# Quarters of the output panels between the attention heads of the last two mixers

## The chip, the cores and the metric

One core of one Trainium2 chip runs the whole program. The metric is the device time of one execution, in microseconds (us). TensorE multiplies, VectorE and ScalarE do the work between the products, GpSimd helps, and SyncE's queue brings the weights.

## The reference, cut to what matters

Two blocks, one behind the other, on 256 tokens of 1024 channels. The first has four gated feed-forward layers and two mixers, and is not touched. The second has two mixers (`l` = 0 and 1) of this form:

```python
for l in range(DEPTH):
    h = rms_norm(x, norm_g[l])
    proj = h @ w_in[l]
    q_a, k_a, v_a, q_h, f_h, i_h, q_m, z = jnp.split(proj, split_points, axis=-1)
    ...
    o_a = moba_attention(qa, ka, va).reshape(B, S, G)
    ...
    o_h = rms_norm(o_h, hgrn_o_norm[l]).astype(x.dtype).reshape(B, S, G)

    kv_m = rms_norm(mem, mem_norm_g[l]) @ w_mem_kv[l]
    ...
    o_m = memory_attention(qm, km, vm).reshape(B, S, G)

    y = jnp.concatenate([o_a, o_h, o_m], axis=-1) * jax.nn.silu(z)
    x = x + y @ w_out[l]
```

`o_a` is causal attention with 8 heads of 64 channels (`moba`), `o_h` a gated recurrence with 4 heads of 128 (`hgrn`), `o_m` attention to 256 rows of memory with 4 heads of 128 (`matt`).

## The kernel before

**Panels.** All weights come as 226 panels of 128 x 2048 numbers (1 MB), in the order in which they are used. Three slots hold them. SyncE loads panel n when panel n - 3 has been split. ScalarE rounds a panel into `w_hi` (`split_hi`, line 1345), VectorE takes the rest into `w_lo` (`split_lo`, line 1638), and TensorE does each product three times (`three`, lines 897 to 899): hi by hi, lo by hi, hi by lo. A panel of a projection or of an output is 48 such products of 128 x 256; in the very last output (`down_rows`) it is 24 of 128 x 512. `split_hi` of panel n waits until TensorE has used panel n - 3.

**The order of the work.** `order()` writes one list of steps, (engine, kind, arguments), and each engine runs its own steps in the order of this list; semaphores count finished steps. So a step that stands early in the list and waits holds everything behind it on its engine.

**The last mixers.** The input projection `in2_l` has 20 panels (numbers 170 to 189 and 200 to 219), the output `out2_l` 6 (190 to 195 and 220 to 225). Panels 4 to 19 of the projection are cut into halves and woven between the rounds of the recurrence (`level` products, line 1093), of the column norms (`cn_sum` line 1237, `cn_rstd`, `cn_use` lines 1882 and 1884) and of the rotations (`swap` line 1226, `rope`). `BESIDE_2` says behind which round each half stands, counted from the round in which the norms begin. The heads run as a pipeline of rounds, 12 heads, `moba` 0 to 7 and then `matt` 0 to 3. In round r, with the step's lag in brackets:

```python
ATTEND = [("pe", "turn_p", 2), ("pe", "scores", 0), ("pe", "attend", 3), ("act", "p_cols", 2), ("dve", "divide", 1),
          ("dve", "mask_max", 0), ("act", "exp", 0)]
```

`scores` (lines 1250, 1252) goes to a PSUM bank, `mask_max` (VectorE, line 1918 or 1916) scales, masks and finds the maximum, `exp` (ScalarE, line 1545), `divide` (VectorE, lines 1931, 1935), `turn_p` transposes (lines 1262 to 1268), `p_cols` (ScalarE, line 1556) copies back, `attend` (lines 1208, 1209) multiplies by the values. When all heads are done, `gate_out` multiplies by the gate, `y_hi` and `y_lo` split the result, and the six output panels follow as whole panels. Beside the heads of mixer 0 the memory rows of mixer 1 are normed (`sumsq`, `row_rstd`, `scale`); beside those of mixer 1 the residual x is turned into rows (`turn_back` line 1065, `rows_back`).

## Time and profile before

| | |
|---|---|
| median of three runs | 1662.78 us (1659.75 to 1663.9) |
| profiled execution, its own time | 1663.09 us |
| its span, first to last instruction | 1660.7 us |
| TensorE busy | 1574.2 us, 95% of the span, 12086 products |
| TensorE loading weights | 1498.2 us, 90% |
| VectorE busy | 1033.9 us, 62% |
| ScalarE busy | 749.7 us, 45% |
| GpSimd busy | 93.5 us, 6% |
| granted clock, mean over the span | 0.971 |
| chain that ended last | TensorE 80%, VectorE 12%, ScalarE 4% |

Busy times are sums over the execution; the engines work beside each other. A busy TensorE need not be a fast one, so the granted clock of each stretch is read beside it.

### The profile page before, as it was taken

The page shows a single profiled execution, that of the slowest core. Times are in us where ns is not written, and L with a number is a line of the kernel's source. Part 1 is how long each engine was busy: PE and PEld are TensorE (multiplying, and loading weights), DVE is VectorE, ACT ScalarE, POOL GpSimd, SP SyncE. Part 2 cuts the span into 40 slices and gives each one's busy share as a digit, 9 for nine tenths or more (in the row PEclk, how much of TensorE's full clock was granted, in tenths as well). Part 3 has the DMA queues.
Part 4 walks back from the last instruction along what each step waited for, and adds up shares of the span by engine and source line. Part 5 has one row for each costly group of instructions (what it writes and reads, how often), then busy time and mean ns, then how long its engine had stood idle before and what let it go on. Part 6 is the DMA issues. An engine that isn't in the chain of part 4 may idle for free.

```text
span 1660.7 us, 28994 instructions
## 1 busy us (share of the span) xinstructions
PE 1574.2 (95%) x12086; PEld 1498.2 (90%) x12086; DVE 1033.9 (62%) x1234; ACT 749.7 (45%) x890; POOL 93.5 (6%) x66
## 2 busy tenths in 40 slices
PE   6999998998999999999997999999999899899988
PEld 6999998887999999999886899999999679799856
DVE  5555577736755575556576755556686655578644
ACT  4333356325433353333446433335645564554653
POOL 1000000010000000000000100002022001013000
PEclk9999999999999999999999999999999889999979
DMA  6554534204554544555331455544444214424201
GB/s 251 191 185 177 179 126 153 87 17 157 201 179 177 180 173 180 183 188 184 137 143 52 167 195 189 182 177 153 152 159 147 76 52 178 177 102 153 102 1 76
DMA packets 34064, 246.53 MB, mean 148 GB/s; under 512 B 3835, under 2 KB 3963, under 8 KB 4406
## 3 DMA queue, kind: packets, MB, share of 16 engines
q1 hardware_dynamic: 32854, 238.28, 39.8%
q0 software_dynamic: 1120, 6.96, 1.1%
q8 instruction: 68, 1.11, 0.3%
q14 instruction: 22, 0.18, 0.0%
HBM read 244.18 MB, written 1.05 MB: 148 GB/s over the span
## 4 chain that ended last, share of the span: by engine, by line
PE 80%; DVE 12%; ACT 4%; issue 2%; DMA 1%; POOL 0%; DVEq 0%; SPq 0%; ACTq 0%; POOLq 0%
PE ps L897 23%; PE ps L899 23%; PE ps L898 23%; PE ps L1093 4%; DVE w_lo L1638 2%; DVE act_lo L1737 2%; ACT act_hi L1414 1%; DVE x L1696 1%; ACT w_hi L1345 1%; PE ps L1237 1%; PE ps L1208 1%; ACT work L1545 1%; PE ps L1252 1%; PE ps L1226 1%; DVE work L1757 1%
## 5 line engine op out<-in xcount | busy, mean ns | idle before, releaser
L897 PE MATMUL ps<-act_hi,w_hi 128*128 128x256 f32 x2528 | 733.5, 290 | 27.6 <-DVE act_lo L1737 9.0
L898 PE MATMUL ps<-act_lo,w_hi 128*128 128x256 f32 x2528 | 722.0, 286 | 0.0
L899 PE MATMUL ps<-act_hi,w_lo 128*128 128x256 f32 x2528 | 721.7, 285 | 0.0
L1638 DVE TENSOR_TENSOR w_lo<-raw,w_hi 128x2048 fp32r<-128x2048 f32 x225 | 526.1, 2342 | 288.0 <-ACT w_hi L1345 285.5
L1345 ACT ACTIVATE w_hi<-raw 128x2048 fp32r<-128x2048 f32 x225 | 429.2, 1910 | 490.9 <-PE ps L899 484.7
L897 PEld LDWEIGHTS ps<-act_hi,w_hi 128*128 128x128 f32 x2528 | 491.9, 195 | 38.0 <-DVE act_lo L1737 11.0
L898 PEld LDWEIGHTS ps<-act_lo,w_hi 128*128 128x128 f32 x2528 | 492.4, 195 | 3.2 <-issue 3.1
L899 PEld LDWEIGHTS ps<-act_hi,w_lo 128*128 128x128 f32 x2528 | 491.8, 195 | 0.0
L897 PE MATMUL ps<-g_hi,w_hi 128*128 128x256 f32 x704 | 199.4, 283 | 0.0
L899 PE MATMUL ps<-g_hi,w_lo 128*128 128x256 f32 x704 | 199.3, 283 | 0.0
L898 PE MATMUL ps<-g_lo,w_hi 128*128 128x256 f32 x704 | 199.3, 283 | 0.0
L897 PEld LDWEIGHTS ps<-g_hi,w_hi 128*128 128x128 f32 x704 | 135.2, 192 | 0.0
L899 PEld LDWEIGHTS ps<-g_hi,w_lo 128*128 128x128 f32 x704 | 135.2, 192 | 0.0
L898 PEld LDWEIGHTS ps<-g_lo,w_hi 128*128 128x128 f32 x704 | 135.2, 192 | 0.0
L897 PE MATMUL ps<-w_hi,act_hi 128*128 128x256 f32 (+1 forms) x336 | 107.3, 319 | 0.0
L898 PE MATMUL ps<-w_lo,act_hi 128*128 128x256 f32 (+1 forms) x336 | 101.2, 301 | 0.0
L899 PE MATMUL ps<-w_hi,act_lo 128*128 128x256 f32 (+1 forms) x336 | 101.0, 301 | 0.0
L881 POOL TENSOR_TENSOR pair<-pair 128x512 f32<-128x512 f32 x27 | 40.7, 1506 | 905.5 <-ACT pair L1392 904.8
L897 PEld LDWEIGHTS ps<-w_hi,act_hi 128*128 128x128 f32 x336 | 65.3, 194 | 5.8 <-issue 3.6
L898 PEld LDWEIGHTS ps<-w_lo,act_hi 128*128 128x128 f32 x336 | 65.3, 194 | 4.8 <-issue 2.9
L1648 DVE TENSOR_TENSOR pair<-ps,r_b 128x512 f32<-128x512 f32 x44 | 30.4, 690 | 60.4 <-PE ps L899 60.4
L899 PEld LDWEIGHTS ps<-w_hi,act_lo 128*128 128x128 f32 x336 | 65.2, 194 | 1.9
(262 smaller groups left out, 1418.9 us busy)
## 6 DMA issues: line engine op xcount, KB each, us to landing
raw<-panels SPq DMA_DIRECT2D x226, 1024.0 KB, 4.8
table<-tab POOLq DMA_DIRECT2D x1, 1472.0 KB, 11.3
table<-tab POOLq DMA_DIRECT2D x1, 1216.0 KB, 5.8
xn<-x_in SPq DMA_DIRECT2D x1, 1024.0 KB, 5.1
work<-mem_in POOLq DMA_DIRECT2D x1, 1024.0 KB, 10.1
xn<-mem_in POOLq DMA_DIRECT2D x1, 1024.0 KB, 5.4
out<-work POOLq DMA_DIRECT2D x4, 256.0 KB, 2.3
table<-tab POOLq DMA_DIRECT2D x1, 832.5 KB, 6.1
```

The costliest lines, as they stand in the source:

```text
L881: nc.gpsimd.tensor_tensor(pair[:, 0:512], pair[:, 0:512], pair[:, 512 * b:512 * b + 512], ALU.add).then_inc(pool_done, 1)
L897: pe.matmul(o, l[0], r[0], start=start, stop=False, skip_group_check=shared)
L898: pe.matmul(o, l[0], r[1], start=False, stop=False, skip_group_check=shared)
L899: return pe.matmul(o, l[1], r[0], start=False, stop=stop, skip_group_check=shared)
L1093: ins = pe.transpose(oh, lhs(h), ident) if turn else pe.matmul(oh, lhs(h), rhs(h), start=True, stop=True)
L1208: pe.matmul(o, v0, first, start=True, stop=False, skip_group_check=True)
L1226: pe.matmul(ps[:, bank], matrix, values, start=True, stop=True).then_inc(pe_done, 1)
L1237: pe.matmul(ps[:, bank], ones, sq[norm_index[unit] % 2], start=True, stop=True).then_inc(pe_done, 1)
L1345: nc.scalar.activation(w_hi[:, s], raw[:, s], ACT.Copy).then_inc(panel_hi, 1)
L1638: tt(w_lo[:, s], raw[:, s], w_hi[:, s].bitcast(F32), ALU.subtract).then_inc(panel_lo, 1)
L1648: tt(grid(gate_x, 2), grid(ps[:, 4], 2), rb(2), ALU.mult).then_inc(gate_scaled, 1)
L1737: finish(stt(act_lo[:, s], src, gain_col(tag, c), act_hi[:, s].bitcast(F32), ALU.mult, ALU.subtract))
```

## The change

- The first four output panels are cut into quarters (`quarter`: the 12 products, or 6 wide ones, that write one of four banks) and one quarter stands behind the `attend` of each round, from round 3 on in mixer 0 and from round 5 on in mixer 1. The quarters that the rounds have no place for follow behind the last head, then panels 4 and 5 whole.
- The last eight halves of the projection (panels 16 to 19) stand two rounds later, so the last three of them are among the first heads. The splits of the panels that follow them go with them.
- The gates and splits of the output rows (`gate_out`, `y_hi`, `y_lo`) stand as single steps between the heads.
- The norm of the memory rows stands as single steps in several rounds instead of in one.
- To leave banks 0 to 3 for the output, scores of all heads from the fourth on go to bank 4 and their turned probabilities to bank 5, one bank each instead of two.
- x is turned into rows in rounds 3 to 6, in banks 0 to 3.

```diff
-def halves(panels):
...
+def halves(panels, bare=2):
...
     out = []
-    panels = panels[:-2] + [p[:2] for p in panels[-2:]]
+    panels = panels[:len(panels) - bare] + [p[:2] for p in panels[len(panels) - bare:]]
     for (_, _, args), *rest in panels:
         out += [[("pe", "half", (*args, 0))], [("pe", "half", (*args, 1)), *rest]]
     return out
...
 BESIDE_2 = [-13, -13, -12, -12, -11, -11, -10, -10, -9, -9, -8, -8, -7, -7, -6, -6, -5, -5, -4, -4, -3, -3, -2, -2,
-            -1, 0, 1, 2, 3, 4, 5, 6]
+            1, 2, 3, 4, 5, 6, 7, 8]
...
     chains = [rounds(NORM_COLS, [(f"sk{l}", 0), (f"sk{l}", 1)]), hgrn,
               [[]] * n + rounds(NORM_COLS, qk + [(f"ho{l}", 0), (f"ho{l}", 1), (f"sq{l}", 0), (f"sq{l}", 1)]),
               [[]] * (n + 2) + rounds(ROPE, qk),
-              [[]] * (h + 11) + [[("dve", "gate_out", ((f"moba{l}", g),)) for g in (0, 1)]],
               [[]] * h + rounds(ATTEND, [(f"moba{l}", i) for i in range(8)] + [(f"matt{l}", i) for i in range(4)]),
-              [[]] * (h + 13) + [y_splits(l, 0), y_splits(l, 2)]]
+              [[]] * (h + 7) + [[("dve", "gate_out", ((f"moba{l}", 0),))], y_splits(l, 0), [], [],
+                                [("dve", "gate_out", ((f"moba{l}", 1),))], y_splits(l, 2),
+                                [("dve", "gate_out", ((f"matt{l}", 0),))], y_splits(l, 8)],
+              [[]] * (h + 3 + 2 * l) + out_pieces(f"out2_{l}", 0, 4)]
     if l == 0:
         load, *stats = mem_norm(1)
-        chains += [[[]] * (h + 1) + [[load]] + [[]] * 3 + [[s for s in stats if s[0] == "act"]] +
-                   [[s for s in stats if s[1] == "scale"]]]
+        chains += [[[]] * (h + 1) + [[load]] + [[]] * 2 + [stats[0:1], stats[1:3], stats[3:4], stats[4:6], [], stats[6:7], stats[7:8]]]
     if l:
-        chains += [[[]] * (h + 2) + sum(([[("pe", "turn_back", (b,)), ("act", "rows_back", (b,))], []] for b in range(PAIRS)), [])]
+        chains += [[[]] * (h + 3) + [[("pe", "turn_back", (b,)), ("act", "rows_back", (b,))] for b in range(PAIRS)]]
     places = [n + r for r in BESIDE_2]
-    out = weave(merge(*chains), halves(panel_list(f"in2_{l}", None, 4)), places)
-    return (out + late_splits(f"in2_{l}") + [("dve", "gate_out", ((f"matt{l}", g),)) for g in (0, 1)]
-            + y_splits(l, 8) + y_splits(l, 10))
+    out = weave(merge(*chains), halves(panel_list(f"in2_{l}", None, 4), 0), places)
+    return out + [("dve", "gate_out", ((f"matt{l}", 1),))] + y_splits(l, 10)
+
+
+def out_pieces(name, start, stop):
+
+    out = []
+    for (_, _, args), *rest in panel_list(name, None, start, stop):
+        pieces = [[("pe", "quarter", (*args, b))] for b in range(PAIRS)]
+        pieces[-1] += rest
+        out += pieces
+    return out
...
-            out += panel_steps("out2_0", None, 0, 4) + turns + all_columns("mem1") + panel_steps("out2_0", None, 4)
+            out += panel_steps("out2_0", None, 4, 5) + turns + all_columns("mem1") + panel_steps("out2_0", None, 5)
...
         else:
-            out += panel_steps("out2_1")
+            out += panel_steps("out2_1", None, 4)
...
+        def first_three(unit):
+
+            return unit[0].startswith("moba") and unit[1] < 3
+
         def score_bank(unit, m, back=False):
 
 
             i = att_index[unit]
             two = lambda u_: len(atts[u_][0]) == 2
+            if unit[0][0] == "m" and not first_three(unit):
+                return 1 if back else 4
             if back:
                 return 1 if two(unit) or (i and two(att_list[i - 1])) else 2
             return m if two(unit) else i % 2
+
+        def turn_bank(unit):
+
+            return 5 if unit[0][0] == "m" and not first_three(unit) else 2 + att_index[unit] % 2
 
         def spans(full):
...
         def back_bank(b):
-            return bank_of("in2_1", b)
+            return b
...
-            def down(slot, parts, first, last, n, j=None, step=0):
+            def down(slot, parts, first, last, n, j=None, step=0, pairs=range(PAIRS)):
 
                 pe.wait_ge(panel_lo, of(j, n + 1, step))
-                for d in range(DC):
+                for d in range(2 * pairs[0], 2 * pairs[-1] + 2):
                     for c in range(2):
                         o = ps[:, d // 2, SEQ * (d % 2):SEQ * (d % 2) + SEQ]
                         ins = three(o, weight(slot, c, P * d, P, D), [a[:, c, :] for a in parts],
                                     first and c == 0 and d % 2 == 0, last and c == 1, True)
                     if last and d % 2 and d < DC - 1:
                         ins.then_inc(bank_ready, 1)
-                ins.then_inc(panel_used, 1)
-
-            def down_rows(slot, parts, first, last, n):
+                if pairs[-1] == PAIRS - 1:
+                    ins.then_inc(panel_used, 1)
+
...
-            def panel(name, k, parts=(0, 1)):
+            def panel(name, k, parts=(0, 1), pairs=range(PAIRS)):
                 n = BASE[name] + k
                 if name.startswith("out"):
 
+                    if (name, k) == ("out2_0", 0):
+                        b = pairs[-1]
+                        e, kind = ("dve", "mask_max") if b < 2 else ("act", "p_cols")
+                        pe.wait_ge(done[e], at(e, kind, ("moba0", 2 - b % 2)))
+                    if (name, k) == ("out2_1", 0):
+                        pe.wait_ge(act_done, at("act", "rows_back", pairs[-1]))
                     last = {("out0", 0): ("cn_use", ("do", 1)), ("out0", 2): ("cn_use", ("ro", 1)), ("out1", 0): ("cn_use", ("fo", 1)), ("out1", 2): ("gate_out", ("dil", 1))}
                     for l in range(2):
-                        last.update({(f"out2_{l}", 0): ("cn_use", (f"ho{l}", 1)), (f"out2_{l}", 2): ("y_lo", l, 2),
-                                     (f"out2_{l}", 4): ("y_lo", l, 10)})
+                        last.update({(f"out2_{l}", 0): ("cn_use", (f"ho{l}", 1)), (f"out2_{l}", 2): ("y_lo", l, 0), (f"out2_{l}", 3): ("y_lo", l, 2),
+                                     (f"out2_{l}", 4): ("y_lo", l, 8), (f"out2_{l}", 5): ("y_lo", l, 10)})
...
-                    (down_rows if name == "out2_1" else down)(n % SLOTS, parts, k == 0, k == N_OF[name] - 1, n)
+                    (down_rows if name == "out2_1" else down)(n % SLOTS, parts, k == 0, k == N_OF[name] - 1, n, pairs=pairs)
...
+            def quarter_panel(name, k, b):
+                panel(name, k, pairs=(b,))
...
                 if b < 2:
-                    pe.wait_ge(act_done, at("act", "evacuate", "in2_1", 18 + b))
+                    pe.wait_ge(dve_done, at("dve", "mask_max", ("moba1", 2 - b)))
                 else:
-                    pe.wait_ge(act_done, at("act", "rows_back", b - 2))
+                    pe.wait_ge(act_done, at("act", "p_cols", ("moba1", 4 - b)))
...
+                if unit[0].startswith("moba") and unit[1] == 3:
+                    pe.wait_ge(act_done, at("act", "evacuate", "in2_" + unit[0][4], 19))
...
+                back = 1 if turn_bank(unit) == 5 else 2
+                if i >= back:
+                    pe.wait_ge(act_done, at("act", "p_cols", att_list[i - back]))
+                p, bank = probs[:, i % 2, 0], ps[:, turn_bank(unit)]
...
-                if unit[0].startswith("matt") and unit[1] == 0:
-                    pe.wait_ge(dve_done, at("dve", "gate_out", ("moba" + unit[0][4:], 1)))
+                if unit[0].startswith("matt") and unit[1] % 2 == 0:
+                    pe.wait_ge(dve_done, at("dve", "gate_out", ("moba" + unit[0][4:], unit[1] // 2)))
```

What this does to VectorE's order at the head of the heads in mixer 0. In the rows, line 1884 (after: 1917) and the three behind it are the norm of the last pair of the recurrence's heads with its split, 1882 (1915) the norm of a memory query, 1918 (1951) mask_max, 1931 and 1935 (1964, 1968) divide, 1638 (1671) split_lo. Before:

```order
L1884 SCALAR_TENSOR_TENSOR xn<-ps,small,pair 128x512
L1886 TENSOR_TENSOR xn<-xn,work 128x512
L1874 CAST act_hi<-xn 128x512
L1875 TENSOR_TENSOR act_lo<-xn,act_hi 128x512
L1882 SCALAR_TENSOR_TENSOR work<-work,small,pair 128x512
L1918 ISA work,stat<-ps,table 128x128
L1918 ISA stat 128x1
L1918 ISA work,stat<-ps,table 128x256
L1918 ISA stat 128x1
L1882 SCALAR_TENSOR_TENSOR work<-work,small,pair 128x512
L1931 RECIPROCAL stat<-stat 128x2
```

and with the change:

```order
L1671 TENSOR_TENSOR w_lo<-raw,w_hi 128x2048
L1917 SCALAR_TENSOR_TENSOR xn<-ps,small,pair 128x512
L1919 TENSOR_TENSOR xn<-xn,work 128x512
L1907 CAST act_hi<-xn 128x512
L1908 TENSOR_TENSOR act_lo<-xn,act_hi 128x512
L1915 SCALAR_TENSOR_TENSOR work<-work,small,pair 128x512
L1951 ISA work,stat<-ps,table 128x128
L1951 ISA stat 128x1
L1951 ISA work,stat<-ps,table 128x256
L1951 ISA stat 128x1
L1671 TENSOR_TENSOR w_lo<-raw,w_hi 128x2048
L1915 SCALAR_TENSOR_TENSOR work<-work,small,pair 128x512
```

The split_lo of panel 190 now stands ahead of that norm, and the one of panel 191 between the first mask_max and the norm that the first divide stands behind.

VectorE again, two rounds on, the mask of head 2 and the divide of head 2. Before:

```order
L1918 ISA work,stat<-ps,table 128x128
L1918 ISA stat 128x1
L1918 ISA work,stat<-ps,table 128x256
L1918 ISA stat 128x1
L1931 RECIPROCAL stat<-stat 128x2
L1935 TENSOR_SCALAR work<-work,stat 128x128
```

and with the change:

```order
L1951 ISA work,stat<-ps,table 128x128
L1951 ISA stat 128x1
L1951 ISA work,stat<-ps,table 128x256
L1951 ISA stat 128x1
L1671 TENSOR_TENSOR w_lo<-raw,w_hi 128x2048
L1964 RECIPROCAL stat<-stat 128x2
```

The split_lo of panel 192 has come between them.

TensorE in round 5 of mixer 1, from the scores to the step behind attend. Line 1250 and 1252 (after: 1282, 1284) are scores, 1208 and 1209 (1238, 1239) attend, 1065 (1095) a transpose of x, 1262 (1295) the next turn. Before:

```order
L1250 MATMUL ps<-work 128x128
L1252 MATMUL ps<-work 128x256
L1208 MATMUL ps<-work 64x256
L1209 MATMUL ps<-work 64x128
L1262 MATMUL ps<-const,work 128x128
```

and with the change:

```order
L1282 MATMUL ps<-work 128x128
L1284 MATMUL ps<-work 128x256
L1238 MATMUL ps<-work 64x256
L1239 MATMUL ps<-work 64x128
L917 MATMUL ps<-w_hi,act_hi 128x512
L918 MATMUL ps<-w_lo,act_hi 128x512
L919 MATMUL ps<-w_hi,act_lo 128x512
L917 MATMUL ps<-w_hi,act_hi 128x512
L918 MATMUL ps<-w_lo,act_hi 128x512
L919 MATMUL ps<-w_hi,act_lo 128x512
L1095 MATMUL ps<-const,x 128x128 x4
```

Six products of an output panel have come behind attend, and behind them the transposes of x.

## Rows read from the trace of the kernel before

**Rows 1.** Windows: stretch, its length, busy time of each engine, PEclk, DMA share, GB/s

```profile
1312.00:1357.00 45.00, 37.27 (x135) 22.84 (x134) 21.99 (x91) 25.57 (x81) 0.33 (x1) 0.70 0.07 24
1357.00:1393.00 36.00, 36.00 (x304) 36.00 (x303) 23.08 (x23) 18.68 (x20) 0.96 (x1) 1.00 0.48 176
...
1623.00:1656.00 33.00, 32.92 (x146) 26.89 (x144) 17.18 (x14) 10.61 (x8) 1.49 (x3) 1.00 0.20 79
```

**Rows 2.** Timeline of TensorE, mixer 0: start, us, instruction, [idle before, releaser]

```profile
1318.38 0.47 PE L1262 MATMUL ps<-const,work 128*128 128x128 f32 x1 [4.83 <-DVE work L1935]
...
1320.98 0.47 PE L1262 MATMUL ps<-const,work 128*128 128x128 f32 x1
...
1328.74 0.48 PE L1262 MATMUL ps<-const,work 128*128 128x128 f32 x1
...
1356.72 0.47 PE L897 MATMUL ps<-act_hi,w_hi 128*128 128x256 f32 x1
```

**Rows 3.** Windows at low clock, and one with half panels between heads

```profile
881.35:884.76 3.41, 3.41 (x15) 2.58 (x15) 1.00 (x1) 2.69 (x4) 0.00 (x0) 0.50 0.26 103
...
1314.84:1342.14 27.30, 23.64 (x68) 13.88 (x69) 11.97 (x54) 15.81 (x52) 0.00 (x0) 0.50 0.06 23
...
883.00:898.00 15.00, 13.51 (x97) 12.93 (x98) 9.46 (x36) 6.69 (x22) 0.00 (x0) 0.94 0.19 70
```

**Rows 4.** Timeline of TensorE, mixer 1, a round at full clock

```profile
1605.28 0.48 PE L1250 MATMUL ps<-work 64*128 64x128 f32 x2
...
1606.13 0.65 PE L1208 MATMUL ps<-work 128*64 128x256 f32 x2
...
1606.92 0.33 PE L1262 MATMUL ps<-const,work 128*128 128x128 f32 x1
...
1607.31 0.60 PE L1250 MATMUL ps<-work 128*128 128x256 f32 x2
```

**Rows 5.** Timeline of TensorE, mixer 0, first product of the recurrence's output

```profile
1281.22 0.38 PE L1310 MATMUL ps<-work 128*128 128x128 f32 x2
```

**Rows 6.** Timeline of VectorE, mixer 0, end of the levels

```profile
1274.84 1.36 DVE L2044 COPY_PREDICATED work<-table,ps 128x512 f32<-128x512 uint32 x2 [1.80 <-PE ps L1093]
1276.24 2.29 DVE L1638 TENSOR_TENSOR w_lo<-raw,w_hi 128x2048 fp32r<-128x2048 f32 x1
1278.55 0.69 DVE L2046 COPY work<-ps 128x512 f32<-128x512 f32 x1
```

**Rows 7.** Timeline of TensorE, the heads of the first block's second mixer

```profile
880.85 0.33 PE L1262 MATMUL ps<-const,work 128*128 128x128 f32 x1 [3.75 <-DVE work L1939]
```

**Rows 8.** Timeline of VectorE, mixer 0, the first heads

```profile
1312.23 0.75 DVE L1882 SCALAR_TENSOR_TENSOR work<-work,small,pair 128x512 f32<-128x512 f32 x1 [0.77 <-ACT pair L1535]
...
1313.24 0.42 DVE L1918 CUSTOM_DVE_ANT_0 work<-ps,table 128x256 f32<-128x256 f32 x1
...
1317.78 0.55 DVE L1935 TENSOR_SCALAR work<-work,stat 128x128 f32<-128x128 f32 x2
```

**Rows 9.** Timeline of ScalarE, mixer 0, exp of head 0 and the evacuate behind it

```profile
1313.70 0.40 ACT L1545 ACTIVATE work<-work,stat 128x128 f32<-128x128 f32 x1 [1.57 <-DVE stat L1918]
...
1314.86 0.60 ACT L1436 ACTIVATE work<-ps 128x512 f32<-128x512 f32 x1 [0.17 <-ACT work L1545]
```

**Rows 10.** The page, costliest groups: the two splits

```profile
L1638 DVE TENSOR_TENSOR w_lo<-raw,w_hi 128x2048 fp32r<-128x2048 f32 x225 | 526.1, 2342 | 288.0 <-ACT w_hi L1345 285.5
L1345 ACT ACTIVATE w_hi<-raw 128x2048 fp32r<-128x2048 f32 x225 | 429.2, 1910 | 490.9 <-PE ps L899 484.7
```

**Rows 11.** Timeline of TensorE, mixer 1: turn of head 0, first output panel

```profile
1584.19 0.48 PE L1262 MATMUL ps<-const,work 128*128 128x128 f32 x1 [4.83 <-DVE work L1935]
...
1622.88 0.59 PE L897 MATMUL ps<-w_hi,act_hi 128*128 128x512 f32 x1
```

**Rows 12.** Timeline of TensorE, two turns with half a panel between (first block)

```profile
893.64 0.27 PE L1262 MATMUL ps<-const,work 128*128 128x128 f32 x1
...
898.15 0.27 PE L1262 MATMUL ps<-const,work 128*128 128x128 f32 x1
```

28 lines of the change are left out of this document (13 added, 15 removed).

## The prediction

> **What bounds the kernel now.** The page says that TensorE is busy nearly all of the time, so I looked for where it is not, or where busy does not mean fast. The table of stretches shows that at once [rows 1]. While the heads of each of the two last mixers run (1312 to 1357 and, in the same form, 1578 to 1623) the granted clock is only 0.70 and TensorE is idle for 7.7 of 45 us, and the DMA engines move almost nothing (0.07). The stretches behind them, the output panels, are dense: 304 panel products in 36.00 us, so 0.118 us each, and 146 wide ones in 32.92 us, 0.225 us each. So the place to win something is inside the heads' stage, and a panel put there costs TensorE 48 x 0.118 = 5.7 us at full clock.
>
> Then the timeline of TensorE there [rows 2]. It waits 4.83 us for VectorE before the turn of head 0 at 1318.38; the turn of head 1 follows at 1320.98, that of head 3 at 1328.74, and the first output panel starts at 1356.72. The row of the clock [rows 3] gives 27.30 us at 0.50, that is 1.2 GHz, with TensorE busy for 23.64 of them. At full clock, 2.4 GHz, a round's products start 0.39 (turn), 0.85 (scores) and 0.79 us (attend) apart, 2.03 us in all [rows 4]: the lost clock costs some 12 us in each mixer, the idle time some 7 us. What limits a round where TensorE doesn't is the loop mask_max, exp, divide: 1320.98 - 1318.38 = 2.6 us [rows 2], of which mask_max is 0.65 (its second part is the row 1313.24, over at 1313.66), divide 0.75 (its last 0.55 in the row at 1317.78) [rows 8], exp 1.0 (from 1313.70, up to the evacuate at 1314.86 less a hop of 0.17) [rows 9].
>
> **The change, part by part, for the first of the two mixers.** Round r is the one with the scores of head r.
>
> *The projection's last halves two rounds later.* Two halves stood before and behind the last level product. Now nothing stands there, and the state product (row 1281.22 [rows 5]) waits only for VectorE: level_in 6 from 1274.84, a split_lo of 2.29, and the copy of level 7, over at 1279.24 [rows 6]. That is 2.0 us earlier, and TensorE idles in front of it, where it was busy: the last level's products can be over 1 us after level 6 is handed on at 1274.84, so some 3.5 us. After the nearest such gap, 3.75 us [rows 7], the clock was 0.50 for 3.41 us [rows 3]. The same here costs 1.7 us. Together -0.3 us. Bounds: -2.0 if the clock holds, +1.4 if it is low twice as long. The rounds behind it keep their shape (half, column sum, swap), one panel later.
>
> *The split of panel 190 and 191 in VectorE's and ScalarE's order.* The order shows a w_lo ahead of the norm of the last HGRN pair and another behind the first mask_max. The first pushes mask_max by 2.29 less the 0.77 us for which VectorE was idle ahead of row 1312.23 [rows 8]: +1.5. The second sits in the chain to the first turn. Before: mask_max ends at 1313.66, the turn starts at 1318.38, 4.7 us. After: exp 1.0, evacuate 0.6 [rows 9], split_hi 1.9, split_lo 2.3 (means of 1.910 and 2.342 us [rows 10]), the norm use 0.75 (as at 1312.23), divide 0.75 [rows 8], hops 0.3: 7.6 us, +2.9. Sum +4.4 us. Cover gone: before, these two splits lay under panel products on TensorE; queued behind the w_lo are divide of head 0 and all masks after it, and TensorE waits for those. The moved half 19 fills 2.9 us of the wait, and this is no gain, as it was taken from the gap of the step before.
>
> *Rounds 2 to 5.* Before: 1318.38 to 1328.74, 10.4 us. After, from the turn of head 0: mask, exp, divide, mask, exp (3.5 us with hops), evacuate 0.6 and split_hi 1.9, split_lo 2.3, divide 0.75 and hops: the turn of head 2 comes at +10.1, mask_max at +10.75; then scores 0.85, attend 0.8, a quarter of 12 x 0.118 = 1.4 with 0.25 for getting into it: round 5 starts at +14.1. So +3.7 us, with two quarters done. The 0.25 is chosen between nothing and the 0.47 us of the first product of row 1356.72 [rows 2].
>
> *Rounds 5 to the end of the heads.* Before: 1328.74 to 1356.72, 28.0 us. After, if the clock is full: a round of 2.03 + 1.65 = 3.7 us; seven of them with 0.3 for the wider products of the memory heads, 26.3; three without scores, 3.1 + 3.1 + 2.4 = 8.6; and stalls. Each w_lo among the heads (193, 194) is asked for when its slot comes free, at the end of a quarter, and then 1.9 + 2.3 + 0.75 us pass to the next divide. A round hides all but some 1.4 to 1.9 us of it; with a short third wait 3.6 us. Sum 38.5: +10.5 us, with ten quarters done.
>
> *The output panels behind.* Twelve quarters are gone: -12 x 1.42 = -17.0 us.
>
> The first mixer: -0.3 + 4.4 + 3.7 + 10.5 - 17.0 = **+1.3 us**.
>
> The second mixer is the same up to its turn of head 0 (-0.3 + 4.4). From there to the first panel it was 1622.88 - 1584.19 = 38.7 us [rows 11]. Now: 13.2 to round 5 (no quarter yet, two transposes of x of 0.5); two rounds with both, 8.3; one of 3.65; four of 3.75 with the wider heads, 15.1; a stall at split 223, 1.8; 5.9 and 0.9 at the end: 48.9, +10.2 us. Nine quarters of 6 x 0.225 = 1.35 are gone: -12.2. Sum **+2.1 us**.
>
> *At nothing.* The memory norm in single pieces is 4.9 us of ScalarE in four parts, at most 1.3 in a round; p_cols and exp take 1.5 of the 3.7, so the round hides it, and if not, it is 1 us per part. The panel loads start earlier with the splits, on SP's queue alone and while the engines carry 0.07 [rows 1]. The score bank shared by all heads from the fourth on makes scores wait for the mask before it; that mask ends some 2 us before TensorE is back from its quarter. The first quarters' waits (mask_max, p_cols or the copied rows) are on steps a round old. Behind a waiting quarter stands the next turn, and for that ScalarE's p_cols waits.
>
> In sum +3.4 us on the profiled execution's 1663.1: 1666.5. That execution lies 0.3 us over the median of the three runs; I say **1666 us**. The kernel's measurement tells a change of 0.3%, 5 us, from none. The idle time is mostly not removed: the filler hides it, and the splits that feed the filler make it anew in the chain of the heads.
>
> **Rivals.** (1) *The filler comes cheaply.* If the clock holds through the new gap (-1.7 each) and getting into and out of a quarter costs nothing (-0.25 for 21 quarters, -5.2), it is 1658 us. For it speaks a head with half a panel between the dilated heads: 898.15 - 893.64 = 4.51 us [rows 12], of which 24 x 0.118 = 2.83 are the panel, so 1.68 for head and transition, under my 2.28. Against it: those heads use 128-wide operands, these 64-wide ones, and three of my rounds are not TensorE's anyway.
>
> (2) *The clock stays low.* It ends on the slower side. TensorE enters round 2 from a wait of nearly 3 us, as now from one of 4.83. If it stays at 1.2 GHz, each round from the fifth costs 3.7 us more, since both head and quarter double. One such round in each mixer gives 1674 us, three 1689; from half a round in one mixer on, it decides for slower. For it: once low in these stages, it stayed so for 27.3 us with TensorE busy [rows 3]. Against it: no dense panel stood in that stretch, and with half panels between the heads the mean was 0.94 from 883 to 898 [rows 3]. The stalls that I count, four in each mixer, are the other way to it: after each a low stretch of 3.41 us, 1.7 us lost, would be +13.6 us, 1680. The Trainium skill has this as a rule: "TensorE: Matmul & The Clock Gate", section "A second HAM failure mode: psum-queue depth-cycling", says that short idles between groups of products, often enough, make the clock go up and down. By that rule the filler with its stalls would not hold the clock; the trace agrees in part, since the stretch from 883 to 898 had a wait of 1.49 us and lost little.
>
> (3) *ScalarE and VectorE set the rounds.* If every split costs what it does in round 3 (4.2 us instead of some 1.7), three of them add 7 us: 1673. Against it: a round has 1.1 us between 3.7 and 2.6, and turns lag by two rounds. That the quarters end up waiting for their own banks, so that nothing is interleaved, I hold for very unlikely, and count it here.
>
> **Chances.** Forecast as worked out, 0.40, with a range of its own of 1661 to 1671; three quarters of it within 0.3%, the rest slower. Rival 1: 0.25, 0.20 of it faster. Rival 2: 0.25, nearly all slower. Rival 3: 0.10, mostly slower. So faster 0.20, same 0.40, slower 0.40. The range takes in rival 1's figure and one low round per mixer: 1657 to 1678; 0.1 is left below, 0.1 above.
>
> **What will show it.** In the changed profile: a TensorE gap of 3 to 4 us before the state products and 0.50 on the clock behind it; the turn of head 0 some 4 us later against its stage; waits of TensorE for divide of 1.5 to 2.3 us after the w_lo among the heads; rounds of 3.7 us between turns; the last head's attend over near 1374 instead of 1356.7 in the first mixer; the clock of the heads' stage above 0.9. Wrong would be: a clock of 0.5 in filled rounds (then slower), rounds near 3.1 us and no stall at the splits (then faster by several us per mixer), or a longer wait of the quarters than of the turns.

## The result, and the profile after

The changed kernel takes 1674.18 us (median of 4 runs, 1673.17 to 1674.65), the kernel before in the same session 1663.09 us: a ratio of 1.0069, 95% interval 1.0048 to 1.0089. It is 11.1 us slower, by more than the 0.3% that a measurement of this kernel can tell from none. The profiled execution took 1674.13 us with a span of 1672.4, against 1660.7 of before. The forecast was 1666 us, with 0.40 each for no measurable change and for slower: it was 8 us too low, and its range, 1657 to 1678, holds the time.

First the stages that answer to [rows 1] and [rows 3], in the table of stretches of the changed kernel (stretch, its length, busy time of PE, PEld, DVE, ACT, POOL, granted clock, DMA share, GB/s):

```profile
1314.90:1373.90 59.00, 49.11 (x286) 38.87 (x285) 31.69 (x93) 32.83 (x81) 0.00 (x0) 0.88 0.23 87
1373.90:1399.00 25.10, 25.10 (x212) 25.07 (x211) 14.43 (x17) 13.11 (x17) 2.50 (x2) 1.00 0.23 85
1399.00:1407.60 8.60, 4.78 (x23) 4.22 (x23) 7.35 (x3) 3.81 (x5) 5.06 (x2) 0.80 0.65 247
1595.33:1615.81 20.48, 17.25 (x51) 10.38 (x50) 8.36 (x32) 9.90 (x28) 0.00 (x0) 0.50 0.23 88
1646.80:1667.60 20.80, 20.78 (x92) 16.87 (x90) 8.03 (x9) 3.18 (x3) 1.43 (x3) 1.00 0.06 24
```

The stretch of the heads has grown and its clock has risen from 0.70 to 0.88, but TensorE still idles for 9.9 us in it. The third row is new: behind the output panels, where before nothing waited, TensorE is busy for 4.78 of 8.60 us. In the last mixer there is still a stretch of 20.48 us at 0.50.

Next the timeline of TensorE in mixer 0, to be laid beside [rows 2] and [rows 5]: the recurrence's output, then the turns (L1295) of heads 0, 1, 3, 4, 6 and 10 and, between the second and the third of them, the scores (L1282) of head 3.

```profile
1279.71 0.49 PE L1343 MATMUL ps<-work 128*128 128x128 f32 x2 [3.53 <-DVE work L2079]
...
1321.23 0.33 PE L1295 MATMUL ps<-const,work 128*128 128x128 f32 x1 [3.19 <-DVE work L1968]
...
1323.83 0.47 PE L1295 MATMUL ps<-const,work 128*128 128x128 f32 x1 [0.97 <-DVE work L1968]
...
1326.33 0.76 PE L1282 MATMUL ps<-work 64*128 64x128 f32 x2 [1.61 <-ACT work L1469]
...
1335.89 0.27 PE L1295 MATMUL ps<-const,work 128*128 128x128 f32 x1
...
1339.49 0.27 PE L1295 MATMUL ps<-const,work 128*128 128x128 f32 x1
...
1348.36 0.33 PE L1295 MATMUL ps<-const,work 128*128 128x128 f32 x1 [1.53 <-DVE work L1968]
...
1367.52 0.33 PE L1295 MATMUL ps<-const,work 128*128 128x128 f32 x1 [2.38 <-DVE work L1968]
```

Why the turns wait stands in VectorE's timeline. The `w_lo` rows are splits in the heads' rounds; behind each stand the norm use or the divide for which TensorE waits.

```profile
1317.43 2.29 DVE L1671 TENSOR_TENSOR w_lo<-raw,w_hi 128x2048 fp32r<-128x2048 f32 x1 [3.69 <-ACT w_hi L1378]
1319.64 0.75 DVE L1915 SCALAR_TENSOR_TENSOR work<-work,small,pair 128x512 f32<-128x512 f32 x1
1320.42 0.17 DVE L1964 RECIPROCAL stat<-stat 128x2 f32<-128x2 f32 x1
1320.62 0.55 DVE L1968 TENSOR_SCALAR work<-work,stat 128x128 f32<-128x128 f32 x2
...
1328.13 2.29 DVE L1671 TENSOR_TENSOR w_lo<-raw,w_hi 128x2048 fp32r<-128x2048 f32 x1 [3.69 <-ACT w_hi L1378]
...
1345.35 2.29 DVE L1671 TENSOR_TENSOR w_lo<-raw,w_hi 128x2048 fp32r<-128x2048 f32 x1 [3.75 <-ACT w_hi L1378]
```

VectorE is not short of time: it stands idle for 3.7 us ahead of each split, because the split's high part is on ScalarE behind the exponential of the same round. What could run meanwhile, the divide at the second and third split, is queued behind.

Last, the tail. In the kernel before, the four residuals ran one by one beside the last output panel, and the norm's sums followed without a wait (VectorE, then TensorE):

```profile
1389.16 0.69 DVE L1696 SCALAR_TENSOR_TENSOR x<-ps,x 128x512 f32<-128x512 f32 x1 [0.69 <-PE ps L899]
...
1393.47 0.69 DVE L1696 SCALAR_TENSOR_TENSOR x<-ps,x 128x512 f32<-128x512 f32 x1 [0.75 <-PE ps L899]
```

```profile
1398.96 0.59 PE L1071 MATMUL ps<-pair,const 128*128 128x256 f32 x2
```

In the changed kernel the transposes and columns of mem1 stand between output panels 4 and 5 (`x_lo`, the row of eight), and the residuals queue behind them; then GpSimd's additions, then TensorE's norm sums:

```profile
1390.02 4.12 DVE L1770 SCALAR_TENSOR_TENSOR act_lo<-ps,gain_c,act_hi 128x256 fp32r<-128x256 f32 x8 [2.20 <-ACT act_hi L1447]
1394.18 2.87 DVE L1729 SCALAR_TENSOR_TENSOR x<-ps,x 128x512 f32<-128x512 f32 x4
1397.08 6.00 DVE L1671 TENSOR_TENSOR w_lo<-raw,w_hi 128x2048 fp32r<-128x2048 f32 x2
```

```profile
1396.35 7.85 POOL L901 TENSOR_TENSOR pair<-pair 128x512 f32<-128x512 f32 x3 [83.21 <-ACT pair L1425]
```

```profile
1404.26 1.22 PE L1101 MATMUL ps<-pair,const 128*128 128x256 f32 x2 [3.82 <-POOL pair L901]
```

**Where the 11.7 us of span are.** The turn of [rows 7] stands at 881.35 instead of 880.85, so 0.5 us of the difference are older than the change. Mixer 0, each step less the one before: the recurrence's output -2.0 (1279.71 against [rows 5]), the turn of head 0 +4.4, that of head 3 +4.3 [rows 2], the quarter behind the last attend, at 1373.88, +10.0, the rest of the output panels -15.9: together +0.8. (This quarter is the twelfth, so eleven stand ahead of that point.) The tail: the norm's sums start 9.8 us behind the last output panel's last product instead of 5.8, +4.0, and enter a stretch of 3.41 us at half clock, +1.7, so +5.7. Between the tail and the recurrence's output of mixer 1 both kernels have 10.24 us at half clock, but at other places (3.41 us from 1455.38 and 6.83 from 1472.45, against 6.83 from 1447.96 and 3.41 from 1468.44): +0.9. Mixer 1, against [rows 11]: -2.0, +4.4 (turn of head 0 at 1594.32), then +13.8 to the quarter behind the last attend at 1646.80 (the tenth; nine stand ahead of it), -12.3: +3.9. The sum, 0.5 + 0.8 + 5.7 + 0.9 + 3.9, is 11.8, with rounding the 11.7.

### The profile page after: what moved, and what is told of

Its sections match the earlier page's. It is cut to its first block, busy times and chain, and to the rows that moved or that the text cites. A ratio compares the mean times of both kernels' runs of the same rounds, so it can differ in the third digit from the quotient of the medians.

```text
span 1672.4 us, 29018 instructions
## 1 busy us (share of the span) xinstructions
PE 1569.3 (94%) x12086; PEld 1495.5 (89%) x12086; DVE 1034.3 (62%) x1234; ACT 749.9 (45%) x890; POOL 95.3 (6%) x66
## 4 chain that ended last, share of the span: by engine, by line
PE 78%; DVE 13%; ACT 5%; issue 3%; DMA 1%; POOL 1%; DVEq 0%; SPq 0%; ACTq 0%; POOLq 0%
PE ps L917 23%; PE ps L919 22%; PE ps L918 22%; PE ps L1123 4%; DVE w_lo L1671 3%; DVE act_lo L1770 2%; ACT w_hi L1378 2%; ACT act_hi L1447 1%; DVE x L1729 1%; PE ps L1238 1%; PE ps L1267 1%; DMA raw<-panels 1%; DVE work L1790 1%; ACT work L1578 1%; PE ps L1284 1%
## 5 line engine op out<-in xcount | busy, mean ns | idle before, releaser
L917 PE MATMUL ps<-act_hi,w_hi 128*128 128x256 f32 x2528 | 737.0, 292 | 30.3 <-DVE act_lo L1770 10.1
L901 POOL TENSOR_TENSOR pair<-pair 128x512 f32<-128x512 f32 x27 | 42.5, 1574 | 907.7 <-ACT pair L1425 907.0
## 6 DMA issues: line engine op xcount, KB each, us to landing
work<-mem_in POOLq DMA_DIRECT2D x1, 1024.0 KB, 10.5
```

The costliest lines, as they stand in the source:

```text
L901: nc.gpsimd.tensor_tensor(pair[:, 0:512], pair[:, 0:512], pair[:, 512 * b:512 * b + 512], ALU.add).then_inc(pool_done, 1)
L917: pe.matmul(o, l[0], r[0], start=start, stop=False, skip_group_check=shared)
```

## The experiments

Each ratio is against the kernel before on the same chip in the same session; there were four sessions, each on another chip, so two experiments are compared by their ratios. The kernel before itself spreads over 1655.8 to 1667.9 us, so ratios are over many runs, and single profiles are read for their stages only. 0.1% is 1.7 us. "The quarter behind the last attend" marks the end of a heads' stage below, as above.

**1. The tail alone.** The one line on the old kernel:

```diff
-            out += panel_steps("out2_0", None, 0, 4) + turns + all_columns("mem1") + panel_steps("out2_0", None, 4)
+            out += panel_steps("out2_0", None, 0, 5) + turns + all_columns("mem1") + panel_steps("out2_0", None, 5)
```

> The kernel before with one line of the change alone: the transposes of x for the second memory norm (turn_x and the column copies of mem1) stand between output panels 4 and 5 of the second-last mixer, not between 3 and 4. Theory (the tail costs): in the changed kernel they put the four residuals one after another behind the last output panel instead of beside it, so that the norm's sums wait for GpSimd's additions and the clock falls to half; nothing of this needs the quarters, so this kernel is slower than the one before by 4 to 6 us (about 1668). Rival (the tail is a consequence of the quarters, and this move costs nothing): within 1 us of the kernel before.

1666.56 us, ratio 1.0037 (1.0022 to 1.0052): 6 us slower by the ratio, 4.4 by the medians. Its profile shows the same wait in front of the norm's sums, with no quarter anywhere:

```profile
1403.82 0.70 PE L1071 MATMUL ps<-pair,const 128*128 128x256 f32 x2 [3.75 <-POOL pair L881]
```

**2. The tail undone in the changed kernel**, with the last heads' gates and y splits as rounds of the chain:

```diff
-            out += panel_steps("out2_0", None, 4, 5) + turns + all_columns("mem1") + panel_steps("out2_0", None, 5)
+            out += turns + all_columns("mem1") + panel_steps("out2_0", None, 4)
...
-                                [("dve", "gate_out", ((f"matt{l}", 0),))], y_splits(l, 8)],
+                                [("dve", "gate_out", ((f"matt{l}", 0),))], y_splits(l, 8),
+                                [("dve", "gate_out", ((f"matt{l}", 1),))], y_splits(l, 10)],
...
-    return out + [("dve", "gate_out", ((f"matt{l}", 1),))] + y_splits(l, 10)
+    return out
```

> The changed kernel with the transposes and column copies of mem1 back between output panels 3 and 4, and with the gates and y splits of the last four heads as rounds of the chain of heads rather than behind everything. Theory (the tail costs about 5.6 us of the 11.1): faster than the changed kernel by 4 to 6 us, about 1669, and still 4 to 7 us slower than before by what the heads' rounds cost. Rival (the quarters in the rounds cost all of it, the tail only moves the wait): within 1.5 us of the changed kernel, about 1674.

1669.53 us, 1.0049 (1.0030 to 1.0068): 0.20% below the changed kernel, 3.3 us, somewhat less than expected. In its profile the norm's sums start at 1397.99 without a wait, and no stretch at half clock follows. But a stretch of 3.41 us at half clock began behind the recurrence's output in both mixers, where the changed kernel's profile has none: from there to the turn of head 0 it is 43.1 us in both instead of 41.5. The gates' and y splits' part of this edit was not run alone.

**3. The halves back** in the changed kernel:

```diff
-            1, 2, 3, 4, 5, 6, 7, 8]
+            -1, 0, 1, 2, 3, 4, 5, 6]
```

> The changed kernel with the last eight projection halves back in the rounds -1 to 6 (the two-rounds-later part undone, the rest kept). Theory (the later halves fill the gap in front of hgrn_out, 2.05 us in each of the two mixers, at no price, since the chain of the first head is set by the splits): slower than the changed kernel by 3 to 4.5 us, about 1678. Rival, the step as the prediction had it (2.0 us gained and 1.7 us lost to half clock without the two last halves in each mixer): slower by 0.5 to 1 us, about 1675. A third, that the low clock of the first rounds comes from the late halves: faster by 1 to 3 us.

1668.54 us, 1.0039 (1.0025 to 1.0054): 5 us faster than the changed kernel. My theory and the prediction's step both fall. The third, that the low clock comes from the late halves, forecast the right side but not the reason: this profile has 17.07 us at half clock in the first rounds of mixer 0, the changed kernel's 10.24, and both have 20.48 in mixer 1. Each half takes along the split of the panel that follows it. Two rounds earlier, the split of panel 191 stands ahead of the first mask_max, and only that of 192 is left in the first heads' chain; from the turn of head 0 to that of head 3 it is then 12.9 us (1323.05 to 1335.95) in mixer 0 instead of 14.7. Mixer 0 ends level all the same, as the gain ahead of the recurrence's output is gone; mixer 1 is 3.4 us shorter (its last attend at 1642.57 instead of 1646.01).

**4. The halves later, alone**, on the kernel before; the two last panels' splits stay behind the heads, as they did there. Same two lines as in 3, with the signs turned.

> The kernel before with one part of the change alone: the last eight projection halves of both last mixers two rounds later (the table's last eight numbers 1 to 8), no quarters. The prediction's step: 2.0 us gained in front of hgrn_out and 1.7 us lost in the first rounds to each mixer, so 0.3 us a mixer and within 1 us of the kernel before. Theory after the undoing of this part made the changed kernel about 5 us faster: the gain in front of hgrn_out is given back because the splits of the first output panels move with the halves into the first heads' chain and the low clock begins later and so ends later; the kernel is 0 to 4 us slower than before. Rival (the halves fill waits at no price): 3 to 4 us faster.

1659.39 us, 0.9986 (0.9970 to 1.0001): some 2 us faster, at the edge of what can be told from none, so the later halves do no harm without the splits and cost with them. The waits ahead of the first turns are nearly gone. The turn of head 0 is no earlier for it: this profile is 3.6 us ahead of the one of before when the last mixers begin, and 2.5 us ahead at this turn.

```profile
1315.91 0.33 PE L1262 MATMUL ps<-const,work 128*128 128x128 f32 x1 [0.42 <-DVE work L1935]
...
1318.50 0.33 PE L1262 MATMUL ps<-const,work 128*128 128x128 f32 x1 [1.20 <-DVE work L1935]
```

The same form of stage then ran once at half clock (mixer 0) and once not (mixer 1); the profiled execution, 1653.64 us, was the fastest of twelve:

```profile
1319.92:1340.40 20.48, 20.48 (x58) 11.71 (x59) 9.80 (x44) 12.62 (x44) 0.00 (x0) 0.50 0.00 1
1578.39:1614.05 35.66, 30.05 (x170) 20.95 (x169) 18.82 (x84) 22.65 (x66) 0.00 (x0) 1.00 0.00 1
```

**5. Both undone** (2 and 3) in the changed kernel.

> The changed kernel with both undone: transposes and column copies of mem1 between output panels 3 and 4, and the last eight halves back at -1 to 6; the quarters, the splits in the rounds and the norm in pieces stay. If the two add (about 4 to 5.6 us each): 1663 to 1665, level with the kernel before, and the quarters are worth nothing by themselves. If both worked through the same low clock: no better than either alone, 1668 to 1669.

1665.72 us, 1.0019 (1.0003 to 1.0034), so 0.50% below the changed kernel, where the two alone gave 0.20% and 0.30%. Within their intervals they add, as two separate mechanisms do. What is left, 0.19% over the kernel before, says that the quarters with whole splits gain nothing there.

**6. The splits in the rounds, no quarters**: experiment 4, the new `halves` and

```diff
-    out = weave(merge(*chains), halves(panel_list(f"in2_{l}", None, 4)), places)
-    return (out + late_splits(f"in2_{l}") + [("dve", "gate_out", ((f"matt{l}", g),)) for g in (0, 1)]
+    out = weave(merge(*chains), halves(panel_list(f"in2_{l}", None, 4), 0), places)
+    return (out + [("dve", "gate_out", ((f"matt{l}", g),)) for g in (0, 1)]
```

> The kernel with the last eight halves two rounds later (e1, 1659.4 us) and one thing more of the change: the splits of output panels 1 and 2 of both last mixers stand in the first heads' rounds, behind the projection halves whose slots they take, as in the changed kernel; no quarters. Theory (these two splits, 1.5 us on ScalarE and 2.3 us on VectorE each, in the chain of the heads are what the changed kernel's first rounds pay for): the turn of head 0 comes 4.4 us later, that of head 3 some 3 us more than that at most; since the late splits lay under products and gave nothing back, 4 to 7 us slower for each mixer than e1, 1667 to 1673. Rival (it is the quarters that cost, these splits lie in waits): within 1.5 us of e1.

1676.96 us, 1.0087 (1.0070 to 1.0104): 1.01%, 17 us, over experiment 4, more than the 8 to 14 us expected, and slower than the whole change. Two splits a mixer did this, each standing in the chain as in the changed kernel. TensorE and VectorE at the second one:

```profile
1331.81 0.47 PE L1262 MATMUL ps<-const,work 128*128 128x128 f32 x1 [3.37 <-DVE work L1935]
```

```profile
1324.68 0.42 DVE L1918 CUSTOM_DVE_ANT_0 work<-ps,table 128x256 f32<-128x256 f32 x1
...
1328.80 2.29 DVE L1638 TENSOR_TENSOR w_lo<-raw,w_hi 128x2048 fp32r<-128x2048 f32 x1 [3.69 <-ACT w_hi L1345]
1331.01 0.16 DVE L1931 RECIPROCAL stat<-stat 128x2 f32<-128x2 f32 x1
```

This profile is 4.9 us behind experiment 4's ahead of the first recurrence's output (1280.39 against 1275.53). With these taken off, the first output panel starts 5.7 us later in mixer 0 (1364.03 against 1353.48), although experiment 4 lost 1.6 us to a stretch at half clock there and this kernel did not. In mixer 1 it is 11.4 us more from the recurrence's output to the first output panel (1553.29 to 1637.21 against 1541.56 to 1614.05): the chain's delay and a clock of 0.50 for 23.89 us, where experiment 4's profile had none. From here to the changed kernel, the quarters, what moved with them and the tail together take 3 us off by the ratios; the tail adds 3 to 6, so the quarters with what moved with them are worth 6 to 9 us.

**7. The splits in parts, in the same places.** Output panels 1 to 3 are split 512 columns at a time, one part in each round:

```diff
+    for i in range(12):
+        n, q = first + i // 4, i % 4
+        after = ("act", "exp", (atts_of(l)[2 + i],)) if 2 + i < 12 else ("act", "p_cols", (atts_of(l)[i],))
+        p = out.index(after) + 1
+        out[p:p] = [("act", "hi_part", (n, q)), ("dve", "lo_part", (n, q))]
...
```

> The changed kernel with the splits of output panels 1, 2 and 3 of both last mixers each cut into four parts of 512 columns, one part in each round of the heads behind the exponential of that round, in place of a whole split (about 1.5 us on ScalarE and 3 us on VectorE) in a single round. Theory (a whole split in a round stands in the chain of a head and lengthens it by its own length, so the turn behind it comes 1.5 to 2.4 us late and the clock falls in the first rounds): the stalls of the turns at the splits go, the first rounds shorten, 3 to 6 us faster than the changed kernel, about 1670. Rival (VectorE is then the bound in every round: the same work plus the fixed cost of each of 24 more instructions): within 1.5 us of the changed kernel or slower by up to 3 us.

1672.6 us, 1.0062 (1.0043 to 1.0081): not to be told from the changed kernel. (The whole splits in these traces take 1.9 us on ScalarE and 2.3 on VectorE, not 1.5 and 3.) The stalls only changed form. Nearly every part still makes VectorE wait behind the exponential of its own round, 20.6 us in all ahead of the twelve parts in mixer 0 and 20.9 in mixer 1, and the divide stands behind the part:

```profile
1330.25 0.70 DVE L1703 TENSOR_TENSOR w_lo<-raw,w_hi 128x512 fp32r<-128x512 f32 x1 [1.87 <-ACT w_hi L1402]
1330.86 0.16 DVE L1998 RECIPROCAL stat<-stat 128x2 f32<-128x2 f32 x1
```

In this round that costs nothing: the turns of heads 2 and 3 stand 3.60 us apart (1331.44, 1335.04), as long as a round with a quarter takes anyway. It costs in the rounds of the memory heads, where turns stand 4.8 to 5.5 us apart and TensorE waits for the divide. VectorE, then TensorE, at the turn of head 9:

```profile
1357.00 0.69 DVE L1703 TENSOR_TENSOR w_lo<-raw,w_hi 128x512 fp32r<-128x512 f32 x1 [1.98 <-ACT w_hi L1402]
```

```profile
1359.26 0.33 PE L1312 MATMUL ps<-const,work 128*128 128x128 f32 x1 [0.58 <-DVE work L2002]
```

**8. TensorE's waits filled, changed kernel.** Products that nothing reads keep the engine busy:

```diff
+            def idle(l, p, n, bank):
+                for _ in range(n):
+                    pe.matmul(ps[:, bank, 0:SEQ], act_hi[:, 0, 0:P], act_hi[:, 0, :], start=True, stop=True)
```

> The changed kernel with products of 256 columns that nothing reads put into TensorE's waits around the first heads: 24 before the turn of head 0, 7 before that of head 1, 12 before the scores of head 3, and in mixer 1 5 more before the turn of head 2 (they fill the measured gaps of 3.2, 1.0, 1.6 and 0.7 us). Theory (these waits bring the clock to half, which then costs in rounds that TensorE sets): the clock stays at 1.0 through the first heads, 2 us less in the second-last and 4 to 6 us less in the last mixer, 6 to 8 us faster than the changed kernel, about 1667. Rival (ScalarE and VectorE set these rounds, so that the low clock costs nothing, or the clock falls all the same): within 1.5 us of it.

1675.09 us, 1.0083 (1.0058 to 1.0107), no gain. The clock did stay up through the first turns in both mixers (0.94 over both stages, below), yet the turn of head 2 came 7.3 us behind that of head 1 and waited 1.51 and 1.95 us for the divide. In mixer 1 these 7.32 us are the same at half clock (changed kernel, 1596.91 to 1604.23) and at full clock here (1601.21 to 1608.53): VectorE's queue sets the pace, and the lost clock costs nothing. Behind that wait the other half of the rival came in, the clock fell after all, now in rounds with a quarter: for 3.41 us in mixer 0, where the turn of head 3 came 5.4 us behind that of head 2 instead of 3.8, and for 6.83 in mixer 1.

```profile
1316.51:1376.22 59.71, 52.59 (x328) 43.29 (x328) 31.68 (x93) 32.61 (x81) 0.00 (x0) 0.94 0.24 85
1592.30:1649.20 56.90, 51.61 (x271) 39.06 (x271) 27.81 (x89) 30.07 (x70) 0.00 (x0) 0.94 0.11 38
```

**9. TensorE's wait filled, kernel before.** 34 such products ahead of the turn of head 0. The edit reached the last mixer alone; in mixer 0 the kernel is the one before.

```diff
+IDLE = [[(("pe", "turn_p", (("moba0", 0),)), 34, 3)], [(("pe", "turn_p", (("moba1", 0),)), 34, 3)]]
```

> The kernel before with 34 such products of 256 columns ahead of the turn of head 0 in both last mixers, where it waits 4.83 us; nothing else. Theory: the clock then does not fall at 1314.84 and 1581.08 us, and rounds that took 3.88 us at half clock take the 2.64 us that the same rounds took at full clock behind it; six to seven rounds in each mixer, so 6 to 8 us less in each: 12 to 16 us faster than before, about 1649. Rival (the rounds without quarters hold TensorE too little, and the clock falls a few rounds later): 0 to 6 us faster. A third (the rounds are set by ScalarE and VectorE): within 1 us.

1656.96 us, 0.9969 (0.9952 to 0.9986), 5 us from one mixer. The profile holds its own control: mixer 0 untouched, then mixer 1.

```profile
1317.44:1344.75 27.31, 23.66 (x68) 13.93 (x69) 11.99 (x54) 15.83 (x52) 0.00 (x0) 0.50 0.05 20
1581.90:1618.91 37.01, 31.24 (x180) 22.17 (x179) 19.00 (x86) 23.16 (x69) 0.00 (x0) 1.00 0.01 1
```

From the turn of head 0 to the first output panel it is 32.1 us (1586.81 to 1618.91) instead of 38.7 [rows 11]. So 6.6 us is the price of the half clock where no split stands in the rounds; the prediction had put it at some 12. The theory's 6 to 8 us for a mixer holds.

**10. Halves later and all waits filled**: experiment 4 with such products, 25 ahead of `hgrn_out`, 3 and 8 ahead of the turns of heads 0 and 1, 2 ahead of those of heads 2 to 6 (in mixer 1 of heads 2, 4 and 6).

> The same kernel (e1) with products of 256 columns that nothing reads in TensorE's remaining waits of both last mixers: 25 ahead of hgrn_out (a wait of 3.5 us), 3 and 8 ahead of the turns of heads 0 and 1, 2 ahead of those of heads 2 to 6. Theory (in e1's profile the clock fell at 1319.92 and cost 5.5 us in mixer 0's rounds against mixer 1's, where it did not fall; and it fell for 3.4 us at each hgrn_out, 1.6 us each): the clock stays at 1.0 in both, 3 to 9 us faster than e1, 1651 to 1656. Rival (the clock falls all the same, since rounds without quarters are too thin for it): within 1.5 us of e1.

1654.24 us, 0.9951 (0.9936 to 0.9965): by the ratios 5.8 us below experiment 4 and 8 below the kernel before. The one low stretch left in the heads' stages follows a wait that only shows at full clock: the memory norm, still in one round, holds `p_cols` back on ScalarE.

```profile
1336.89 1.04 PE L1214 MATMUL ps<-work 128*64 128x256 f32 x2 [2.63 <-ACT work L1566]
```

The changed kernel, with the norm in single pieces, has no such wait.

**11. Parts in other places, and the waits filled.** The quarters of the change, experiment 2's tail, the products that nothing reads, and the parts of 7 at other places: the low part stands behind the mask_max of the round after its high part's. The high parts begin one round later, the rounds of heads 8 to 10 hold two each, and the whole split of output panel 4 stands right ahead of that of panel 5.

```diff
+    units = atts_of(l)
+    for i in range(12):
+        n, q = first + i // 4, i % 4
+        at_ = 3 + i if i < 8 else i
+        out.insert(out.index(("act", "exp", (units[at_],))) + 1 + (i >= 8 and i < 11), ("act", "hi_part", (n, q)))
+        if at_ < 11:
+            out.insert(out.index(("dve", "mask_max", (units[at_ + 1],))) + 1 + (i >= 8 and i < 11), ("dve", "lo_part", (n, q)))
+        else:
+            out.insert(out.index(("dve", "divide", (units[11],))) + 1, ("dve", "lo_part", (n, q)))
+    for s in splits(first + 3):
+        out.remove(s)
+    p = out.index(("act", "split_hi", (first + 4,)))
+    out[p:p] = splits(first + 3)
...
```

> The changed kernel with its quarters kept, the transposes of mem1 early (b1), and the splits of output panels 1 to 3 in parts of 512 columns: the high part behind an exponential on ScalarE, the low part behind the mask_max of the next round on VectorE, in the 1.87 us that VectorE waits there anyway; and products that nothing reads in the waits ahead of hgrn_out, of the turns of heads 0 and 1 and of the scores of head 3. Theory (the interleaving is sound and only its splits and the half clock cost): every round with a quarter takes 3.6 us, 12 of them and two short ones make about 49 us from head 0's turn to the first remaining quarter, where before it was 38.3 and 17.0 us of quarters behind: 5 to 7 us less in each mixer than before, 1649 to 1655. Rival (quarters between heads cost what they save, whatever the splits do): 1660 to 1667.

1647.66 us, 0.9914 (0.9898 to 0.9929): 15 us faster than the kernel before, the best here. VectorE, then the turns of heads 3, 4 and 5 on TensorE:

```profile
1331.62 0.29 DVE L2000 CUSTOM_DVE_ANT_0 work<-ps,table 128x128 f32<-128x128 f32 x1 [1.09 <-PE ps L1312]
...
1332.30 0.69 DVE L1718 TENSOR_TENSOR w_lo<-raw,w_hi 128x512 fp32r<-128x512 f32 x1
1333.37 0.17 DVE L2013 RECIPROCAL stat<-stat 128x2 f32<-128x2 f32 x1 [0.37 <-ACTq L1620]
```

```profile
1330.15 0.27 PE L1327 MATMUL ps<-const,work 128*128 128x128 f32 x1
...
1333.75 0.27 PE L1327 MATMUL ps<-const,work 128*128 128x128 f32 x1
...
1337.33 0.27 PE L1327 MATMUL ps<-const,work 128*128 128x128 f32 x1
```

The part no longer waits: VectorE's waits ahead of the twelve parts come to 0.35 us in mixer 0 and 0.32 in mixer 1, where experiment 7 has 20.6 and 20.9. VectorE is idle for 0.37 us behind the part shown: the divide waits for its exponential and for nothing else. Rounds with a quarter take 3.6 to 4.4 us, but for one of 6.2 in mixer 0 (TensorE waits 2.36 us there ahead of a quarter), and both stages run at full clock:

```profile
1314.74:1365.14 50.40, 46.49 (x307) 38.33 (x307) 30.57 (x101) 33.65 (x90) 0.00 (x0) 1.00 0.21 80
1573.86:1619.96 46.10, 45.32 (x251) 34.74 (x250) 28.98 (x99) 30.00 (x79) 0.00 (x0) 1.00 0.13 47
```

**12. The same without products that nothing reads.**

> The kernel k1_parts_fill (1647.7 us) without its products that nothing reads: the changed kernel with the transposes of mem1 early and the splits of output panels 1 to 3 in parts placed in waits of ScalarE and VectorE; it computes nothing that is not needed. Theory (the placing of the splits is the larger part, the quarters themselves keep TensorE busy enough that the clock falls only around the first heads' waits of 1.2 and 2.2 us and at hgrn_out): 2 to 6 us slower than with them, 1650 to 1654, still faster than before. Rival (without the filling the clock stays at half for 10 to 20 us in each mixer as in the changed kernel): 1657 to 1663, no better than before.

1655.82 us, 0.9950 (0.9939 to 0.9962), 8 us faster than before, with no work that is not needed. Against experiment 2 (1.0049), whose quarters and tail it shares, cutting and moving the splits is worth 1%; cutting alone (experiment 7) was worth nothing that can be told. Against experiment 11 it loses 0.36%, 6 us, more than I gave it at the centre: its profile has 6.83 us at half clock in mixer 0 and 10.24 in mixer 1, and from the turn of head 0 to the quarter behind the last attend it takes 49.4 and 46.4 us, instead of 46.8 and 42.5.

## Why the prediction was right or wrong

**The splits in the chain, +4.4: right**, +4.4 in both mixers, with the rows it was built from (mask_max, exp, evacuate, split_hi, split_lo, norm use, divide). The two shares came as said: the first split pushes mask_max by 1.6 us (said 1.5), and from its end to the turn it is 7.5 us (said 7.6). *Rounds 2 to 5*, +3.7, were +4.3. The sum had the divide of head 2 over at +10.1, and it was over at +9.9 (1331.09), although its first term was too small (mask_max, exp, divide, mask_max and exp at 3.5 us, where its own prices add up to 4.05 and the trace has 4.3). What it lacked is the first quarter at half clock, behind which that turn came at 1332.08. Experiment 6 shows the mechanism by itself, 5.7 us in mixer 0 with no quarter in the rounds.

**The filled rounds: right.** 3.6 us between turns (1335.89 to 1339.49), said 3.7; stalls of 1.53 and 2.38 us behind the later splits, said 1.4 to 1.9; the prediction's stretch ends behind the twelfth quarter (1375.50), and to there it was +11.6, said 10.5, and -17.5 for the rest, said -17.0. Part of the 1.1 us is a stretch of 3.41 us at half clock from 1349.57, behind the stall of 1.53 us. Mixer 0 came out at +0.8, said +1.3, and only because the recurrence's step gave -2.0 for -0.3.

**The step that failed: "At nothing" and "the output panels behind".** The sum takes 17.0 us off behind the heads and has no term for the transposes and columns of mem1, which the same edit moves from between output panels 3 and 4 to between 4 and 5. That puts 4.12 us of VectorE's work between the last panel and the residuals; what is late next is the residuals, GpSimd's additions (7.85 us for three against 6.03 before: two of them, and not one, now start beside a split that VectorE has begun), and the norm's sums. It is 5.7 of the 8 us by which the sum was short, and experiment 1 measured 6.2 us (0.37%, 3.7 to 8.6) for it alone. The rest is +1.8 in mixer 1, +0.9 ahead of its recurrence's output, +0.5 older than the change and -0.5 in mixer 0. The order of instructions showed the move; I priced only moves ahead of the heads.

**The halves later, -0.3: mis-sized, and wrong about what it hangs on.** The gap came as said, 3.53 us, but the clock did not fall behind it, so the step gave 2.0 us in each mixer. Alone, on the kernel before, the edit is worth 2 us or so, if anything (experiment 4). Within the change it costs 5 us (experiment 3), since every half pulls a split two rounds further into the heads. The prediction had put this under the splits and not seen that the two are one choice.

**The clock: rival 2 was partly true.** In mixer 0 the 10.24 us at half clock lie in rounds that VectorE sets, except for the first quarter, which cost 1.0 us. That a stall brings a low stretch came true once in three stalls of the filled rounds (1.53 us, then 3.41 at half clock; none behind those of 2.38 and 1.85). In mixer 1 the half clock reaches into the filled rounds: turns of heads 3 and 4 stand 7.10 us apart (1609.02, 1616.12), the next two 4.03 (1620.15). Those 3.1 us are most of the 3.6 by which the stretch from the turn of head 0 to the quarter behind the last attend passed its +10.2 (+13.8); the 1.7 us gained at the recurrence hid half of it, so that mixer 1 was +3.9 for +2.1. Rival 1's time (1658) fell. Its first condition came true in this profile, the clock held through the gap in both mixers; of its second about half did, since a round of 3.59 us less 2.03 for the head and 1.42 for the quarter leaves 0.14 us for getting in and out, between its nothing and the 0.25 of the sum. That the time still came out high is the tail, the first rounds and the clock in mixer 1. Rival 3 fell for the filled rounds, but its mechanism, ScalarE and VectorE as the bound, is what sets the first rounds, up to the turn of head 2, as experiment 8 shows.

**What it was about.** "The filler hides it, and the splits that feed the filler make it anew" holds. The runs add that this is a matter of place, not of amount: VectorE has the time for the splits in every round, and experiments 7 and 12 do the same splitting in the same pieces, one at 1.0062 and the other at 0.9950, of which the mended tail is 0.2 to 0.4%. That it is the low part's distance from its high part rests on the traces (VectorE's waits ahead of the parts, 41.4 us against 0.7 over both mixers); no run moved the low parts alone, and in 12 the high parts and the split of panel 4 stand elsewhere too.

Experiment 2's smaller gain (3.3 against the tail's 5.7 us by trace) fits the two stretches at half clock in its profile, 1.6 us each, that the changed kernel's profile lacks; whether the other runs differ in this way is open. Whether another place for the first whole split, that of panel 190, would give more was not tried.

## What to carry to other kernels

A cross-engine pair (high part on one engine, low part on the next) is better issued a round apart, as in experiments 11 and 12, on the two in-order queues: the consumer goes behind work of the next round, into a wait that exists anyway; if it stands behind a partner that is itself waiting, it blocks everything queued after it, however little it takes. Before filling TensorE's idle time with real work, price what feeds the filler and where that stands in the other queues; and when an edit moves a step, follow the chain at its new place up to the next point where TensorE waits, even if that is far behind the stage being tuned. Where rounds are bound by TensorE at half clock, a few products in the one long wait ahead of them are cheap to try (5 us for one line here); where another engine's queue binds, they bring nothing by themselves (experiment 8).
